# Re-ordering the paired products of an output projection, with one weight difference moved to GpSimd

## What is computed

```python
cat = jnp.concatenate([
    od.reshape(B, S, W_DIFF) * jax.nn.silu(gd),
    ow.reshape(B, S, W_DIL) * jax.nn.silu(gw),
    om.reshape(B, S, W_MEM) * jax.nn.silu(gm)], axis=-1).astype(dtype)
y = y + jnp.einsum('bse,ed->bsd', cat, w_out)        # output projection, residual
y_prompt = rms_norm(y_prompt, g_final)               # y * rsqrt(mean(y*y) + EPS) * g
y_sample = rms_norm(y_sample, g_final)
```

## Time and profile before

| | us |
|---|---|
| median of 3 runs | 1076.11 (1075.07 to 1077.32) |
| the profiled execution | 1074.16 |
| its span in the trace | 1072.4 |

### The profile page before, as it was taken

One profiled execution on the slowest core, in us unless ns is written; L12 is line 12 of the kernel. 1 busy time (PEld: TensorE's weight loads), 2 busy tenths in 40 slices (PEclk: granted clock), 3 DMA queues, 4 the chain that ended last, 5 costly groups with the idle time before them and its releaser, 6 DMA issues.

```text
span 1072.4 us, 24077 instructions
## 1 busy us (share of the span) xinstructions
PE 1006.5 (94%) x8074; PEld 980.4 (91%) x8074; DVE 734.0 (68%) x2699; ACT 456.2 (43%) x1192; POOL 55.0 (5%) x126
## 2 busy tenths in 40 slices
PE   4999999999999999999999999979999998999885
PEld 4999999999998999989999999969999997989884
DVE  4673222777788878778777757558775797877773
ACT  5673222223333323343344542314666465445553
POOL 0100000000000000000000000000000201000002
PEclk9999999999999999999999999999999999999998
DMA  8964333889877888767766659788664244322253
GB/s 229 275 179 125 95 89 87 266 264 297 254 243 210 258 267 241 223 208 230 215 215 217 188 180 292 214 261 264 208 210 130 85 153 149 87 80 80 79 158 159
DMA packets 264397, 205.42 MB, mean 192 GB/s; under 512 B 19594, under 2 KB 218826, under 8 KB 262858
## 3 DMA queue, kind: packets, MB, share of 16 engines
q1 hardware_dynamic: 264274, 203.89, 63.1%
HBM read 192.07 MB, written 11.76 MB: 190 GB/s over the span
## 4 chain that ended last, share of the span: by engine, by line
PE 71%; DVE 9%; DMA 7%; ACT 5%; issue 4%; SPq 3%; POOL 1%; DVEq 0%; POOLq 0%; ACTq 0%
PE z L1045 54%; PE z L1071 7%; DVE w_lo L1599 2%; ACT w_hi L1282 2%; DMA pages<-in_cache_mem_k_dram 2%; PE s_ps L1104 1%; DVE pages L1780 1%; PE o_ps L1141 1%; PE t_ps L1091 1%; ACT rows L1510 1%; DMA pages<-in_cache_v_diff_dram 1%; SPq L789 1%; DMA w_raw<-in_w_out_dram 1%; DMA w_raw<-in_w_mem_kv_dram 1%; PE t_ps L1131 1%
## 5 line engine op out<-in xcount | busy, mean ns | idle before, releaser
L1045 PE MATMUL z<-act_hi,w_hi 128*128 128x260 f32 (+2 forms) x2048 | 448.4, 293 | 10.2 <-DVE w_lo L1599 9.8
L1045 PE MATMUL z<-act_hi,w_lo 128*128 128x260 f32 (+2 forms) x2048 | 429.0, 283 | 0.0
L1045 PE MATMUL z<-act_lo,w_hi 128*128 128x260 f32 (+2 forms) x2048 | 428.2, 283 | 0.0
L1045 PEld LDWEIGHTS z<-act_hi,w_hi 128*128 128x128 f32 x2048 | 325.4, 190 | 16.0 <-DVE w_lo L1599 8.5
L1045 PEld LDWEIGHTS z<-act_lo,w_hi 128*128 128x128 f32 x2048 | 323.7, 189 | 0.0
L1045 PEld LDWEIGHTS z<-act_hi,w_lo 128*128 128x128 f32 x2048 | 323.1, 189 | 0.0
L1599 DVE TENSOR_TENSOR w_lo<-w_raw,w_hi 128x512 fp32r<-128x512 f32 x316 | 215.4, 687 | 129.5 <-ACT w_hi L1282 127.7
L1282 ACT ACTIVATE w_hi<-w_raw 128x512 fp32r<-128x512 f32 x316 | 194.8, 626 | 220.0 <-PE z L1045 172.0
L1780 DVE CUSTOM_DVE_ANT_0 pages<-pages,q_bc 128x128 f32<-128x128 f32 x640 | 144.5, 286 | 49.7 <-DMA pages<-in_cache_k_win_dram 20.9
L1809 DVE SCALAR_TENSOR_TENSOR v_acc<-pages,dec_a,v_acc 128x256 f32<-128x256 f32 x224 | 94.1, 478 | 2.5 <-DMA pages<-in_cache_v_diff_dram 2.2
L1408 ACT ACTIVATE probs<-probs,st_n 128x128 f32<-128x128 f32 (+3 forms) x48 | 26.8, 558 | 88.4 <-DVE st_n L1719 88.1
(11 more groups left out here) (211 smaller groups left out, 1066.5 us busy)
## 6 DMA issues: line engine op xcount, KB each, us to landing
w_raw<-in_w_in_dram SPq DMA_DIRECT2D x224, 256.0 KB, 4.3
pages<-in_cache_k_diff_dram SPq DMA_DIRECT2D x128, 256.0 KB, 4.4
pages<-in_cache_v_diff_dram SPq DMA_DIRECT2D x128, 256.0 KB, 3.4
w_raw<-in_w_out_dram SPq DMA_DIRECT2D x72, 256.0 KB, 3.2
w_raw<-in_w_mem_kv_dram SPq DMA_DIRECT2D x32, 256.0 KB, 4.4
cat<-in_x_prompt_dram SPq DMA_DIRECT2D x8, 1024.0 KB, 7.5
q_bc<-q_rows_dram SPq DMA_DIRECT2D x32, 256.0 KB, 6.6
pages<-in_cache_mem_k_dram SPq DMA_DIRECT2D x16, 256.0 KB, 6.6
```

The source lines that it names most:

```text
L1045: last = nc.tensor.matmul(zb[:, bank, 0:b - a], lhs[:, w], rhs[:, kt, a:b], start=(kt == 0 and m == 0), stop=(kt == KT - 1 and m == 2))
```

## The change

It has seven parts. (1) The products of a pair are taken in the order A11, A12, S1, S2, S3, S4, A22. (2) The sums of weights stand in other turns, one a turn, and the loads of a pair in another order (`RAW_ORDER`). (3) S3 is made by GpSimd, with a semaphore of its own. (4) The seven additions stand in other turns, two of them together behind operations 8 and 10, and the half banks are handed out in another cycle. (5) The squares are a job of their own, `ysq`, two turns behind the addition of the residual, which itself stands one or two turns later. (6) Only blocks 0 and 1 are multiplied by the gain tile by tile; blocks 2 and 3 get it in their normalization, four half blocks of 1024 columns, all on DVE. (7) In `raw_loads` the name `at` is set again to the turn in which a place comes free, before it is used for the load's own turn.

```diff
-PRODUCTS = (("A11", "B11"), ("A12", "B21"), ("S2", "T2"), ("S1", "T1"), ("S3", "T3"), ("S4", "B22"), ("A22", "T4"))
+PRODUCTS = (("A11", "B11"), ("A12", "B21"), ("S1", "T1"), ("S2", "T2"), ("S3", "T3"), ("S4", "B22"), ("A22", "T4"))
-SUMS_AT = (("S1", 0, -1), ("S2", 0, 0), ("S1", 1, 0), ("S2", 1, 1), ("S3", 0, 3), ("S3", 1, 4), ("S4", 0, 5), ("S4", 1, 6))
+SUMS_AT = (("S1", 0, -1), ("S1", 1, 0), ("S2", 0, 1), ("S2", 1, 2), ("S3", 0, 4), ("S3", 1, 5), ("S4", 0, 6), ("S4", 1, 7))
+PARTS_AT = (("c1", 2), ("C11", 4), ("U", 8), ("X", 8), ("V", 10), ("C22", 10), ("C12", 12), ("C21", 14))
-RAW_ORDER = (("A11", 0), ("A11", 1), ("A12", 0), ("A21", 0), ("A22", 0), ("A12", 1), ("A21", 1), ("A22", 1))
+RAW_ORDER = (("A11", 0), ("A11", 1), ("A21", 0), ("A22", 0), ("A12", 0), ("A21", 1), ("A22", 1), ("A12", 1))
@@ raw_loads
-                    j = SUM_TURN[last]
-                    gone.append((first + SUMS_AT[j][2], slot, ("sum", len(SUMS_AT) * k + j + 1)))
+                    at = first + SUMS_AT[SUM_TURN[last]][2]
+                    if what == "A12":
+                        gone.append((at, slot, ("sum", SUMMED[k, "S4", i])))
+                    else:
+                        gone.append((at, slot, ("sum3", SUMMED[k, "S3", i])))
@@ Y_NAT_AT
-    if UNIT_OF[n] not in PAIR_AT or e > LAST_PAIRED - 2:
+    if UNIT_OF[n] not in PAIR_AT:
         return DONE[n] + 1
-    return DONE[n] + (7 if e % 2 else 4)
+    if e > LAST_PAIRED - 2:
+        return DONE[n] + (3 if e % 2 else 1)
+    return DONE[n] + (9 if e % 2 else 5)
@@ plan
             put(Y_NAT_AT(n), "ynat", n, 0.8)
+            put(Y_NAT_AT(n) + (2 if c == 0 else 0), "ysq", n)
             if (h, c) == (KT - 1, 1):
                 put(s + 2, "mean", 0)
-                put(s + 4, "norm", 0)
-                for k, later in enumerate((2, 3, 5, 6)):
+                for k in range(4):
+                    put(s + 4 + k, "norm", (2 + k // 2, k % 2))
+                for k, later in enumerate((2, 3, 6, 7)):
                     put(s + later, "ys", k)
-    rank = {"evac": 0, "part": 0, ...
+    rank = {"ynat": 5.5, "norm": 8, "evac": 0, "part": 0, ...
@@ product_bank
-    turn = len(PRODUCTS) * k + p
-    return turn // 2 % 2, turn % 2
+    a, b, c = ((0, 1, 2), (2, 0, 1), (1, 2, 0))[k % 3]
+    return divmod((a, b, c, 3, a, b, 3)[p], 2)
@@ SP
-                    if kind == "norm":
-                        store_y(2)
-                        store_y(3)
+                    if kind == "norm" and what[1]:
+                        store_y(what[0])
@@ vector
-                a, b = Y_BLOCKS[c][0], Y_BLOCKS[c][-1] + 1
-                tile = nat[:, a:b, cols]
+                tile = nat[:, 0:2, cols]
+            def norm(i, half):
+                cols = slice(half * D_MODEL // 2, (half + 1) * D_MODEL // 2)
+                dve.wait_ge(s_yrp, 1)
+                nc.vector.scalar_tensor_tensor(nat[:, i, cols], nat[:, i, cols], y_r[:, i:i + 1], g_fin[:, cols],
+                                               ALU.mult, ALU.mult).then_inc(s_ydone[i], 1)
@@ gpsimd
+            def weight_sum(k, j):
+                name, i, _ = SUMS_AT[j]
+                if name != "S3":
+                    return
+                pool.wait_ge(s_sum, SUMMED[k, "S2", i])
+                pool.wait_ge(s_lo, SPLIT_AT[k, "S1", i] + 1)
+                a11, a21 = (wait_raw(pool, LOAD_OF_RAW[k, w, i]) for w in ("A11", "A21"))
+                nc.gpsimd.tensor_tensor(w_sum[:, SUM_SLOT["S3"] + i, :], a11, a21, ALU.subtract).then_inc(s_sum3, 1)
```

More of the change, by code:

```diff
@@ L316, in plan @@
             put(START[u] + turn, "sum", (k, j))
-        for part in range(7):
-            put(START[u] + 2 * part + 2, "part", (k, part))
+        for part, turn in PARTS_AT:
+            put(START[u] + turn, "part", (k, part))
     put(DONE[AT["qd", 3, 1]] + 1, "qrows", 0)
@@ L1449, in slot @@
                         evac(what)
-                    elif kind == "part" and what[1] == 0:
+                    elif kind == "part" and what[1] == "c1":
                         part_copy(what[0])
@@ L1979, in slot @@
                         weight_sum(*what)
-                    elif kind == "part" and what[1]:
+                    elif kind == "part" and what[1] != "c1":
                         part_out(*what)
@@ L2001, in slot @@
                         y_add(what, use)
-                        if what > FIRST_OUT and TILES[what - 1] != ("y", KT - 1, 1):
+                        if what > FIRST_OUT and TILES[what - 1][2] != 1:
                             times_g(what - 1)
@@ L2080, in slot @@
                         sample_rstd(s_ysn)
+                    elif kind == "sum":
+                        weight_sum(*what)
                     elif kind == "ynat" and TILES[what][2] != 2:
```

75 lines of the change are left out of this document (37 added, 38 removed).

## The result

| | us |
|---|---|
| median before, 4 runs | 1075.59 (1074.86 to 1077.32) |
| median after, 4 runs | 1065.49 (1064.99 to 1069.22) |
| ratio | 0.9911, 95% interval 0.9886 to 0.9937 |
| forecast | 1069.8 (1065.0 to 1077.0) |
| the profiled execution after | 1069.22, its span 1067.4 |

In the changed kernel lines stand 9 to 16 further down than before: paired products L1086, plain ones L1060, squares L1524, additions to the residual L1939, residual transfers L955.

What follows compares the result with a forecast made beforehand. In the output projection no engine was full; the order, with stalls around ACT's squares, was taken to cost. Terms -12.4 + 3.6 - 1.7 + 4.2 = -6.3 us gave 1067.9 profiled, 1069.8 us as median, range 1065.0 to 1077.0.

Steps and rivals of the forecast that it cites:

- The steady pair: Output projection's pairs: PE runs through at 21.08 us a pair instead of 23.78; over five periods a gain of 12.4 us.
- the 17.1 of the sum: DVE's work in a steady pair, forecast to fall from 18.81 us to about 17.1.
- the 19.3 with the blocking: DVE's load in a steady pair, some 19.3 of 21.1 us, if GpSimd's S3 and DVE exclude each other.
- S3 on GpSimd: Weight difference in the pairs: about 1.1 us on GpSimd, ends 0.6 and 3.06, in time for ACT.
- The sum: Whole kernel: -12.4 + 3.6 - 1.7 + 4.2 = -6.3 us.
- I charge nothing: Pairs' turns 3 and 4: DVE time stolen by S3 costs nothing, since a `w_lo` there may be 1.5 us late.
- The first pair: All eight loads stand behind the residual's 4 MB; PE stands 7.1 us before the first paired product; cost 3.6 us.
- 911.9 + 1.0 - 909.3 = 3.6: First pair's cost in us: operation 11's new start plus a half-clock charge, less its start before; range 1 to 6.
- The 1.0 us in it for the half clock: First pair, operations 0 to 2: slow matmuls after PE's idle cost about 1 us, range 0 to 3.
- Behind the pairs: Plain products: a 1.35 us stall goes with the squares and some 0.35 of another 0.56; gain 1.7 us.
- The end: After the last product: half-block multiplications and later rows cost 1.5 us, one more MB stored 2.7; cost 4.2 us.
- the runs shown have a median 2 us above it: Final step for the whole kernel: from 1067.9 us for the profiled execution to a forecast median of 1069.8.

Runs made afterwards that it cites:

- experiment 5: The changed kernel with the squares of the paired tiles back in the turn of the addition to the residual: 1088.02 us, ratio 1.0125.
- experiment 6: The kernel before with only the squares of the paired tiles moved two turns behind the addition to the residual: 1054.80 us, ratio 0.9814.
- experiment 3: The changed kernel with S3 made by DVE in the same turns instead of by GpSimd: 1069.26 us, ratio 0.9949.
- experiment 2: The changed kernel with the paired part's loads planned as in the kernel before (`at` not overwritten): 1060.82 us, ratio 0.9864.
- experiment 8: The kernel before with squares two turns later and `at` overwritten, so all first-pair loads stand behind the residual: 1064.64 us, ratio 0.9898.
- experiment 11: The changed kernel with loads planned as before and end stores reordered (block 3, eight rows, blocks 0 and 1, eight rows): 1059.09 us, ratio 0.9847.
- experiment 12: The kernel before with squares two turns later, blocks 0 and 1 stored in halves, 12 small rows ahead and 4 behind: 1057.32 us, ratio 0.9833.

## Why the prediction was right, and where only its sum was

**The steady pair** was right: 21.08 us forecast, 21.02 measured, no idle PE, and ACT idle ahead of the squares only twice behind the first pair (0.59 and 0.44 us). Experiments 5 and 6 show the cause: the squares' turn, and nothing else. I had given the gain to the change as a whole, and a reader could take from it that the reordering helps; it doesn't. DVE is busy 18.40 us of a pair, between the 17.1 of the sum and the 19.3 with the blocking.

**S3 on GpSimd** was sized at 1.1 us and took 1.68 (1.29 where it meets no DVE instruction with two SBUF inputs in progress). The sum was not touched, as forecast, because S3 has lead. "I charge nothing" was right only against the kernel before; experiment 3 shows that in the new order the move gives 1.7 us by the yardstick and 2.9 by the medians. The trace shows the blocking, up to 1.1 us a time.

**The first pair** was right in its cause: a gap of 7.21 us (7.1 forecast), `w_lo` of operations 1 and 2 about 3 us apart (3.19 and 2.91), half clock behind the gap. Two things in the subtraction "911.9 + 1.0 - 909.3 = 3.6" are wrong. It takes 909.28 for the start of operation 11, and it is that of operation 12. The count of matmuls says so, twelve for an operation: from the first paired one to there, and to the matching place (916.85) in the changed kernel, 144 each (windows of the paired products alone, columns as for the first pair above):

```profile
884.60:909.20 24.60, 19.28 (x144) 1.00 0.48 151
894.50:916.80 22.30, 20.34 (x144) 0.90 0.47 125
```

Set right, the first pair costs 1.44 us more, 5.1, and the five periods behind it, which began at the same misread row, gain 1.44 more, 13.9; the sum doesn't move. Measured from the residual's issue, operation 12 starts 5.0 us later (38.0 against 33.0), and the rest of the pairs takes 13.7 less. The 1.0 us in it for the half clock came true by luck: PE lost 2.3 us in operations 0 and 1, but all of it in time in which it would have waited for `w_lo` (it still stood 0.23 and 0.65 us), and a wait of 0.59 us ahead of operation 12, which I hadn't seen, took its place. Nor does a granted clock of 1.00 at the kernel's start, where the matmuls are 0.21 us apart, show the lower level there; behind the gap the 0.50 does.

The other fault is what the term was taken for: it nets the late loads against the old first pair's stalls. These would have gone with the squares in any case. The sum is the same, but the edit's own price is 7.1 to 8.4 us (experiments 2 and 8), and the squares' own gain is 19.2 (experiment 6: 196.1 - 176.9), not 12.4 + 1.7.

**Behind the pairs** -1.7 was forecast and -2.4 came. Experiment 6 gives 1.6 for the squares. The other 0.8 are waits of 0.56 and 0.25 us in experiment 6 (PE for `ys_n` and for an addition to the residual) of which the changed kernel has only one of 0.23. I put that down to the gain multiplications, which no longer stand ahead of them; no run tests it alone.

**The end** was forecast at +4.2 and came at +3.5: the rows start 1.3 us later against the last product (1.5 forecast), and a MB costs 2.5 (2.7 forecast). The small difference left is the rows' issue, 6.04 instead of 6.30 us.

**The sum** by structure was -7.5 for -6.3. The median came 4.3 us below the forecast, 1.2 of it from the terms. The rest is the step "the runs shown have a median 2 us above it", which carried an offset of a few runs upstream over to the new kernel; the new runs fell the other way. That the median still lies in the range is partly luck: such offsets are as large as the term errors.

By parts, in the yardstick of the table, the change is then: squares -19.2, late loads +7.1 (experiment 2), the rest of the order and S3 +2.1 in the pairs (131.7 of experiment 2 less 129.6), gain multiplications (argued) -0.8, end +3.4. That is -7.4. The new order alone has no run of its own.

## What to carry over

When an in-order engine waits for another inside a job that is not urgent, put the job a turn or two behind its input before touching anything else: here those few lines alone give twice the whole change. Price each edit against the kernel that it will stand in, not against the one that it leaves: costs hidden by a stall come back in full when the stall goes. And where executions differ by microseconds ahead of the part that is changed, compare from an event just in front of it.

## What was not expected of the hardware

- One 128x512 difference took 1.29 us on GpSimd by itself and 0.69 on DVE; begun inside a DVE instruction with two SBUF inputs it took 1.68, and the next such instruction on DVE 1.78 instead of 0.68.
- After 7.2 us of idle PE, the first matmul of 260 columns took 0.59 us and the next ones 0.42, at a granted clock of 0.50, and the first of the group that began 3.2 us later 0.58 (0.78 over that group); after 1.2 us of idle the first took 0.39 and the rest 0.28.
- The issue of a 4 KB row took 0.30 us on SP at the median, but up to 1.23 us while blocks were in flight: 0.38 to 0.48 us on average over 8 to 16 rows that began beside or behind the stores of blocks 2 and 3, and 0.73 to 0.77 right behind the last 2 MB (experiments 11 and 12).
- Ahead of the output projection the granted clock of 100 us stretches was 1.00 in some executions and 0.97 or 0.98 in others. All six with 0.98 in 300 to 400 us issued the residual at 877.2 to 881.9, the eight others at 875.8 to 877.6; what is cause and what effect is open.
